# Second block: the value projections of all heads ahead of the head loop, tokens as rows

## The chip, the cores and the metric

One core of a Trainium2 chip runs the whole kernel in one launch. The metric is the device time of that launch in microseconds. TensorE (PE) does the matmuls, VectorE (DVE) and ScalarE (ACT) the elementwise work, SyncE (SP) and GpSimd (POOL) issue the DMAs. A matmul here takes a stationary tile of 128x128 and streams up to 512 columns past it.

## The reference, cut to what matters

Two transformer-like blocks run one after the other on 512 tokens of width 2048. The change lies in the second:

```
h = rms_norm(x, norm_g)
qa, ka, va, ga, qb, kb, vb, gb = split(h @ w_in)      # 8 parts, each 8 heads of 128
ya = stick_breaking_attention(qa, ka, va)             # per head, causal, blocks of 128 queries
yb = chunk_band_attention(norm(qb), norm(kb), vb)     # per head, 512 tokens, softmax with a bias
x  = x + concat(ya * silu(ga), yb * silu(gb)) @ w_out
```

`va` and `vb` are the value projections; no norm or nonlinearity stands between them and the attention weights, only the rms factor of each token.

## The kernel before, in words

All products are made of float32 split into a high and a low half; a product is three matmuls (high by high, high by low, low by high). A weight unit is 16 tiles of 128x128, 1 MB. SP loads it (`load`, `one_load`) into one of two raw buffers, ScalarE copies its high half (`hi`, L450, four pieces), VectorE subtracts the low half (`lo`, L893, four pieces), and TensorE runs `gemm`: 16 k-steps (k-tiles) of three matmuls of 512 columns into one of two PSUM banks, with the weights as stationary operand, so that the result has features as rows and tokens as columns. The next unit's halves are made while a unit runs; both must be there before its matmuls. `unit` counts finished units, `evac` emptied banks.

The first block ends with an output product of 16 units (`U_O1`). Then comes the second block's head loop (`d2_head` in each engine's program): 8 heads of 8 units each, in the order A queries, A keys, A values, A gate, B queries, B keys, B values, B gate. Each engine's order is written by hand; waits are semaphores. Between k-steps of `gemm` TensorE puts the head's attention matmuls: `scores` A after 2 k-steps of unit 3, `values` A in unit 5, a sum of squares (`b_ss`, 64-row halves folded by VectorE, L1475 to L1477) after 8 k-steps of units 5 and 6, scores B after 14 of unit 6, values B of the head before after 10 of unit 1.

Values come out of `gemm` with tokens as columns, but `values` needs tokens as rows. So VectorE turns them in 32x32 squares (`turn_values`, L1392), and SP sends them to DRAM and back in another order (`regroup`); ScalarE and VectorE then split them (`value_hi`, L796, `value_lo`, L1396). The attention weights of A and B take the same way (`turn_weights`, L1401 and L1403, `regroup`, `weight_hi`, L801, `weight_lo`, L1409): VectorE turns, SP writes to DRAM, waits for the landing, reads back, ScalarE copies, VectorE subtracts.

A's stick-breaking weights are made block by block: ScalarE takes Abs, Exp and Ln of the scores (L821 to L823), VectorE runs five operations with a scan in them (L1457 to L1462, called a stick below), ScalarE an Exp. B's queries and keys are normed: VectorE evacuates (L1473), ScalarE squares, VectorE folds, TensorE sums over the head, ScalarE takes the inverse root, VectorE scales (L1487 to L1490), ScalarE copies the high half, VectorE subtracts the low one (L1492); then come scores B.

The first block's gMLP has a value projection too, with four units that run the other way: activations stationary, weights streaming, tokens as rows, a bank for each 128 tokens.

Of the kernel before, what the change touches and what calls it, by code (L numbers as in the profile page):

```python
# [12 lines left out]
P = 128  # L13
S = 512
# [18 lines left out]
U_D2 = U_O1 + KT  # L33
U_O2 = U_D2 + 8 * DN
# [9 lines left out]
VALUES_AT = 12  # L44
LATE_VALUES_AT = 10
FIRST_VALUES_AT = 15
# [43 lines left out]
def build(nc, w, w_ab, xT, memT, rows_in, consts, negatives, params, ws_t, bs_b, ln_rows, rel, x1_dram, rows_dram, way_v, way_w, outT):  # L90
    with ExitStack() as ctx:
# [53 lines left out]
        QA, KA, VA, SGA = (tl(i) for i in (4, 5, 6, 8))  # L145
# [5 lines left out]
        QB, KBN, VBT, SGB, BIAS = (tl(i) for i in (18, 19, 20, 22, 23))  # L151
        PB = LB
        VTH, VTL = vtok_t[:, 0:S], vtok_t[:, S:2 * S]
        VTURN, VRAW = tl(7), tl(21)
# [34 lines left out]
        chunk_bank = [bank[1], pb[2], pb[3], pb[4]]  # L189

# [37 lines left out]
        def v3(a):  # L228
# [21 lines left out]
            turned v_turn va_in vb_in w_turn aw_in bp_in v_hi a_vtok a_hi a_lo a_z a_l a_x a_w a_wh a_wl a_o  # L250
# [8 lines left out]
        def _(sp):  # L259
# [180 lines left out]
        def _(act):  # L440
# [332 lines left out]
            hi(U_D2, U_D2 % 2)  # L773
# [9 lines left out]
            act.wait_ge(sem["unit"], U_D2)  # L783
            for k in range(12, KT - 1):
                x1_hi(k)
            act.wait_ge(sem["evac"], U_D2)
            x1_hi(KT - 1)
            o1_squares(KT - 1)
            hi(U_D2 + 1, (U_D2 + 1) % 2)
# [4 lines left out]
            def value_hi(ready, n):  # L794
                act.wait_ge(sem[ready], n)
                A(in_order(VTH, NB), by_row(VRAW, NB), ACT.Copy).then_inc(sem["v_hi"], 1)  # L796
# [6 lines left out]
            def d2_head(h, tail=True, last=False):  # L803
                u = 8 * h + U_D2
# [3 lines left out]

                if tail:
                    weight_hi("bp_in", 64 * h)  # L810

                for j in range(3):
                    next_hi(j)
                    if j < 2:
                        act.wait_ge(sem["evac"], u + (j + 1))
                        A([QH, KH][j], [QA, KA][j], ACT.Copy).then_inc(sem["a_hi"], 1)

                for i, c in enumerate(reversed(range(NB))):
# [5 lines left out]
                next_hi(3)  # L824
                for i, c in enumerate(reversed(range(NB))):
# [3 lines left out]
                sigmoid("g_y", 2 * h + 1, "g_sig")  # L829
                value_hi("va_in", 64 * h + 64)  # L830

                for j in range(2):
                    act.wait_ge(sem["evac"], u + (5 + j))
                    A(SQ[0:H, :], Y[0:H, :], ACT.Square)
                    A(E[0:H, :], Y[H:P, :], ACT.Square).then_inc(sem["b_sq"], 1)
                    if j == 0:
                        weight_hi("aw_in", 64 * h + 64)
                    next_hi(4 + j)

                    rsqrt(E, pb[5][:, :], -1.0 / P, "b_ss", 2 * h + j + 1, "b_r")  # L840
                    act.wait_ge(sem["b_n"], 2 * h + j + 1)
                    A([QH, KH][j], [QB, KBN][j], ACT.Copy).then_inc(sem["b_hi"], 1)
                for c in range(NB):
                    pc = PB[:, DO[c]:DO[c] + DNN[c]]
                    act.wait_ge(sem["b_max"], NB * h + c + 1)
                    A(pc, pc, ACT.Exp, bias=small[:, c:c + 1], accum_out=small[:, 4 + c:5 + c]).then_inc(sem["b_exp"], 1)
                next_hi(6)
                value_hi("vb_in", 64 * h + 64)
# [4 lines left out]
                if last:  # L853
# [13 lines left out]
                next_hi(7)  # L867
# [16 lines left out]
        def _(dve):  # L884
# [487 lines left out]
            lo(U_D2, U_D2 % 2)  # L1372
# [6 lines left out]
            lo(U_D2 + 1, (U_D2 + 1) % 2)  # L1379
# [8 lines left out]
            dve.wait_ge(sem["o1_st"], 16 * KT)  # L1388


            def turn_values(src):
                V.transpose(by_row(VTURN, NB), src).then_inc(sem["v_turn"], 1)  # L1392

            def value_lo(n, done):
                dve.wait_ge(sem["v_hi"], n)
                V.tensor_tensor(in_order(VTL, NB), by_row(VRAW, NB), in_order(VTH, NB).bitcast(F32), ALU.subtract)\  # L1396
                    .then_inc(sem[done], 1)

            def turn_weights(src, c):
                n = min(c + 1, NB - 1)  # L1400
                ins = V.transpose(by_row(SPB, SLOTS)[:, c:c + 3 * n - 2:3], src[:, DO[c]:DO[c] + n * P])  # L1401
                if c == NB - 1:
                    ins = V.transpose(by_row(SPB, SLOTS)[:, 7:8], src[:, DO[c] + n * P:DO[c] + DNN[c]])  # L1403
# [8 lines left out]
            def d2_head(h, tail=True, last=False):  # L1412
                u = 8 * h + U_D2
# [17 lines left out]
                if tail:  # L1431
                    gate_silu(2 * h, SGB)
                    weight_lo(4 * h - 2)

                for j, dst in enumerate((QA, KA, VA)):
                    unit(u + j)
                    V.scalar_tensor_tensor(dst, bank[slot(j)][:, :], SCALE if j == 0 else 1.0, R12, ALU.mult, ALU.mult)\  # L1437
                        .then_inc(sem["evac"], 1)
                    if j == 2:
                        dve.wait_ge(sem["evac"], u + 3)  # L1440
                        turn_values(VA)
                    next_lo(j)
                    if j < 2:
                        dve.wait_ge(sem["a_hi"], 2 * h + j + 1)
                        V.tensor_tensor([QL, KL][j], dst, [QH, KH][j].bitcast(F32), ALU.subtract).then_inc(sem["a_lo"], 1)
                    if j == 0 and tail:
                        dve.wait_ge(sem["b_o"], h)
                        out = (h + (DN - 1)) * S
                        out = big[:, bass.ds(out, S)] if not isinstance(out, int) else big[:, out:out + S]
                        V.tensor_tensor(out, pb[4][:, :], SGB, ALU.mult).then_inc(sem["mixed"], 1)  # L1450
                        dve.wait_ge(sem["mixed"], 2 * h + M1)

                for i, c in enumerate(reversed(range(NB))):
# [9 lines left out]
                gate_in(3, SGA)  # L1463
                next_lo(3)
                for i, c in enumerate(reversed(range(NB))):
                    dve.wait_ge(sem["a_w"], NB * h + i + 1)
                    ins = turn_weights(WB, c)
                ins.then_inc(sem["w_turn"], 1)
                gate_silu(2 * h + 1, SGA)
                value_lo(2 * h + 1, "a_vtok")  # L1470
# [613 lines left out]
```

## Time and profile before

| what | value |
|---|---|
| runs of the kernel before (3) | median 1888.71 us, 1887.75 to 1888.98 |
| the profiled execution | 1888.65 us, span 1887.0 us |
| granted TensorE clock, whole span | 1.000 |
| TensorE busy | 1880.1 us of the span |
| VectorE busy, ScalarE busy | 1203.0 us, 819.9 us |
| matmuls | 8912 |

The span runs from the first to the last instruction of the profile. Matmuls are pipelined and their ends are modelled: a row's duration of 0.39 us is longer than the step from one start to the next, so the step is what a matmul costs in a stream. "Idle before" in square brackets is time in which the engine stood still ahead of a row, with what ended it.

### The profile page before, as it was taken

The page shows a single profiled execution, that of the slowest core. Times are in us where ns is not written, and L with a number is a line of the kernel's source. Part 1 is how long each engine was busy: PE and PEld are TensorE (multiplying, and loading weights), DVE is VectorE, ACT ScalarE, POOL GpSimd, SP SyncE. Part 2 cuts the span into 40 slices and gives each one's busy share as a digit, 9 for nine tenths or more (in the row PEclk, how much of TensorE's full clock was granted, in tenths as well). Part 3 has the DMA queues.
Part 4 walks back from the last instruction along what each step waited for, and adds up shares of the span by engine and source line. Part 5 has one row for each costly group of instructions (what it writes and reads, how often), then busy time and mean ns, then how long its engine had stood idle before and what let it go on. Part 6 is the DMA issues. An engine that isn't in the chain of part 4 may idle for free.

```text
span 1887.0 us, 26887 instructions
## 1 busy us (share of the span) xinstructions
PE 1880.1 (100%) x8912; PEld 1564.5 (83%) x8912; DVE 1203.0 (64%) x2246; ACT 819.9 (43%) x1581; POOL 112.4 (6%) x172
## 2 busy tenths in 40 slices
PE   9999999999999999999999999999999999999999
PEld 8788888888888888888888888888888888888887
DVE  6565687788777865734467575757575757576333
ACT  5654444444444444533444343434343535354111
POOL 0100011101111010010000000000000000000100
PEclk9999999999999999999999999999999999999999
DMA  9722233223232212334433434343434333333441
GB/s 331 296 90 83 82 82 88 78 78 78 78 94 74 77 67 100 129 139 144 148 114 113 140 120 147 114 143 116 138 122 135 126 132 125 135 121 134 149 151 67
DMA packets 56146, 230.25 MB, mean 122 GB/s; under 512 B 7073, under 2 KB 23073, under 8 KB 35617
## 3 DMA queue, kind: packets, MB, share of 16 engines
q1 hardware_dynamic: 46224, 194.01, 29.2%
q0 software_dynamic: 9728, 35.49, 6.7%
q8 instruction: 30, 0.49, 0.1%
q14 instruction: 20, 0.16, 0.0%
q10 hardware_dynamic: 144, 0.10, 0.0%
HBM read 207.13 MB, written 22.45 MB: 122 GB/s over the span
## 4 chain that ended last, share of the span: by engine, by line
PE 93%; DVE 3%; DMA 2%; ACT 1%; issue 0%; SPq 0%; DVEq 0%; ACTq 0%
PE gemm L1582 80%; PE pb L1582 12%; DMA raw<-in_w 1%; DVE w_lo L893 1%; PE pb L1585 1%; DMA way_w<-scratch 1%; DMA scratch<-way_w 0%; DVE scratch L1460 0%; ACT w_hi L450 0%; DVE scratch L1461 0%; DVE scratch L1457 0%; DVE w_lo_t L1409 0%; DVE scratch L1401 0%; DVE scratch L1458 0%; SPq L306 0%
## 5 line engine op out<-in xcount | busy, mean ns | idle before, releaser
L1582 PE MATMUL gemm<-act_hi,w_hi 128*128 128x512 f32 x2304 | 918.6, 399 | 0.0
L1582 PE MATMUL gemm<-act_lo,w_hi 128*128 128x512 f32 x2320 | 903.0, 389 | 0.2 <-DVE w_lo L893 0.2
L1582 PE MATMUL gemm<-act_hi,w_lo 128*128 128x512 f32 x2304 | 899.1, 390 | 0.0
L1582 PEld LDWEIGHTS gemm<-act_hi,w_lo 128*128 128x128 f32 x2304 | 432.4, 188 | 92.9
L1582 PEld LDWEIGHTS gemm<-act_lo,w_hi 128*128 128x128 f32 x2320 | 436.5, 188 | 84.7 <-ACT w_hi L450 0.5
L450 ACT ACTIVATE w_hi<-raw 128x512 fp32r<-128x512 f32 x616 | 337.2, 619 | 379.9 <-PE gemm L1582 360.4
L1582 PEld LDWEIGHTS gemm<-act_hi,w_hi 128*128 128x128 f32 x2304 | 433.3, 188 | 82.1 <-issue 0.4
L893 DVE TENSOR_TENSOR w_lo<-raw,w_hi 128x512 fp32r<-128x512 f32 x624 | 399.1, 696 | 151.1 <-ACT w_hi L450 145.2
L1582 PEld LDWEIGHTS pb<-scratch 128*128 128x128 f32 x932 | 135.9, 192 | 27.2 <-DVE scratch L1264 5.9
L1582 PE MATMUL pb<-scratch 128*128 128x128 f32 (+3 forms) x932 | 141.8, 279 | 2.6 <-DVE scratch L908 1.7
L1437 DVE SCALAR_TENSOR_TENSOR scratch<-gemm,scratch 128x512 f32<-128x512 f32 x24 | 16.6, 692 | 95.9 <-PE gemm L1582 95.9
L390 POOL TENSOR_TENSOR scratch<-scratch,cst 128x256 f32<-128x256 f32 x56 | 47.6, 855 | 416.2 <-DVE scratch L1155 243.3
L457 ACT ACTIVATE scratch<-scratch 128x512 f32<-128x512 f32 x56 | 35.2, 628 | 79.0 <-DVE scratch L1104 44.0
L1103 DVE SCALAR_TENSOR_TENSOR scratch<-scratch,par 128x511 f32<-128x511 f32 (+2 forms) x72 | 54.0, 750 | 9.9 <-DVE scratch L1101 3.2
L469 ACT ACTIVATE scratch<-pb,eps 128x512 f32<-128x512 f32 x41 | 28.1, 686 | 69.6 <-PE pb L1582 69.6
L765 ACT ACTIVATE scratch<-big 128x512 f32 (+1 forms) x16 | 10.1, 632 | 108.3 <-DVE big L1351 108.3
L1351 DVE TENSOR_TENSOR big<-gemm,scratch 128x512 f32 (+1 forms) x16 | 11.0, 689 | 68.5 <-PE gemm L1582 68.5
L646 ACT ACTIVATE scratch<-pb 128x128 f32<-128x128 f32 x40 | 11.1, 278 | 91.0 <-PE pb L1582 90.6
L423 POOL DMA_DIRECT2D scratch<-in_rel x7 | 3.8, 540 | 638.7 <-DVE scratch L1500 638.7
L1409 DVE TENSOR_TENSOR w_lo_t<-scratch,w_hi_t 128x640 fp32r<-128x640 f32 x30 | 23.4, 822 | 27.1 <-ACT w_hi_t L801 27.1
L801 ACT ACTIVATE w_hi_t<-scratch 128x640 fp32r<-128x640 f32 x30 | 20.5, 731 | 42.7 <-DMA scratch<-way_w 42.7
L458 ACT ACTIVATE scratch<-scratch 128x512 f32<-128x512 f32 x56 | 35.4, 633 | 1.8
(299 smaller groups left out, 1658.1 us busy)
## 6 DMA issues: line engine op xcount, KB each, us to landing
raw<-in_w SPq DMA_DIRECT2D x154, 1024.0 KB, 4.8
way_w<-scratch SPq DMA_DIRECT2D x15, 640.0 KB, 5.0
scratch<-way_w SPq DMA_DIRECT2D x60, 160.0 KB, 3.1
scratch<-in_rows_in POOLq DMA_DIRECT2D x6, 1024.0 KB, 8.3
big<-in_xT POOLq DMA_DIRECT2D x4, 1024.0 KB, 7.8
scratch<-rows POOLq DMA_DIRECT2D x16, 256.0 KB, 6.1
scratch<-in_xT POOLq DMA_DIRECT2D x16, 256.0 KB, 2.9
x<-big POOLq DMA_DIRECT2D x16, 256.0 KB, 2.3
```

Source lines behind the costliest of these rows:

```text
L390: nc.gpsimd.tensor_tensor(v3(blk(ML, NB * (k % 2), 2)), pair(AT, 0), C[f"level{k}"].rearrange("p (c t) -> p c t", c=1).broadcast_to([P, 2, ...
L450: A(w_hi[slot][:, c], raw[slot][:, c], ACT.Copy).then_inc(sem["hi"], 1)
L457: st.then(A(E, SS, ACT.Exp, scale=-1.0))
L458: st.then(A(E, E, ACT.Ln, bias=1.0))
L469: st.then(A(dst, src, ACT.Ln, bias=eps[:, 0:1], scale=scale))
L801: A(in_order(WBH, SLOTS)[:, s], by_row(WB, SLOTS)[:, s], ACT.Copy).then_inc(sem["a_wh"], 1)
L893: V.tensor_tensor(w_lo[slot][:, c], raw[slot][:, c], w_hi[slot][:, c].bitcast(F32), ALU.subtract)\
L1103: st.then(V.scalar_tensor_tensor(Y[:, 3 - k:], SS[:, :S - 3 + k], tap(k), Y[:, 3 - k:], ALU.mult, ALU.add))
L1409: V.tensor_tensor(in_order(WBL, SLOTS)[:, s], by_row(WB, SLOTS)[:, s], in_order(WBH, SLOTS)[:, s].bitcast(F32), ALU.subtract).then_inc(sem ...
L1437: V.scalar_tensor_tensor(dst, bank[slot(j)][:, :], SCALE if j == 0 else 1.0, R12, ALU.mult, ALU.mult)\
L1582: return nc.tensor.matmul(out, a, b, start=start, stop=stop, skip_group_check=skip)
L1585: return nc.tensor.transpose(out, a, C["ident"])
```

## The change

The two value projections leave the head loop. A new stage of 16 units (`U_VP`) runs between the first block's output product and the head loop: four groups (A's values of heads 0 to 3, of 4 to 7, B's likewise), each of four units. In a unit (`value_unit`) the split activations are stationary and the weights stream, 512 columns for four heads at once; the result has tokens as rows, in four banks for four blocks of tokens, with two sets of four banks in turn. ScalarE empties a group's four banks into `big` with the rms factor of each token as scale (`R12C`, made by VectorE from the broadcast row). `big` held x1, whose stores must have landed.

The head loop has six units: A queries, A keys, B queries, B keys, A gate, B gate. Values are read from `big` when their head comes; their turning and their trips through DRAM go away. Scores A now stand after 5 k-steps of unit 2, the sums of squares after 8 of units 3 and 4, scores B after 14 of unit 4, values A after 4 of unit 5. VectorE evacuates B's queries between the second and the third stick, and the two gates are taken later. ScalarE's copies of A's weights, and VectorE's subtraction, stand ahead of the keys' norm. SP loads two units, sends A's weights round, loads three, sends B's round, and loads one.

```diff
-U_D2 = U_O1 + KT
-U_O2 = U_D2 + 8 * DN
+U_VP = U_O1 + KT
+U_D2 = U_VP + 4 * NB
+U_O2 = U_D2 + 6 * DN
-VALUES_AT = 12
+SCORES_AT = 5
+VALUES_AT = 4
...
 (SyncE, per head)
-                u = U_D2 + 8 * h + 4
+                u = U_D2 + 6 * h + 4
                 one_load(u)
                 one_load(u + 1)
-                sp.wait_ge(sem["v_turn"], 2 * h + 1)
-                regroup(VRAW, VTURN, way_v, 4 * h + 1, "va_in")
+                sp.wait_ge(sem["w_turn"], 2 * h + 1)
+                regroup(WB, SPB, way_w, 2 * h + 1, "aw_in")
                 one_load(u + 2)
                 one_load(u + 3)
-                sp.wait_ge(sem["w_turn"], 2 * h + 1)
-                regroup(WB, SPB, way_w, 4 * h + 2, "aw_in")
                 one_load(u + 4)
-                one_load(u + 5)
-                sp.wait_ge(sem["v_turn"], 2 * h + 2)
-                regroup(VRAW, VTURN, way_v, 4 * h + 3, "vb_in")
-                one_load(u + 6)
                 if h < DN - 1:
                     sp.wait_ge(sem["w_turn"], 2 * h + 2)
-                    regroup(WB, SPB, way_w, 4 * h + 4, "bp_in")
-                one_load(u + 7)
+                    regroup(WB, SPB, way_w, 2 * h + 2, "bp_in")
+                one_load(u + 5)
...
 (ScalarE, the new stage)
+            for n in range(4):
+                u = U_VP + 4 * n
+                for j in range(3):
+                    hi(u + j + 2, (u + j) % 2)
+                if n == 0:
+                    act.wait_ge(sem["o1_st"], 16 * KT)
+                    act.wait_ge(sem["act_lo"], 4 * KT)
+                    act.wait_ge(sem["r12c"], 1)
+                act.wait_ge(sem["unit"], u + 4)
+                heads = big[:, 4 * n * S:(4 * n + 4) * S].rearrange("p (h x) -> p h x", x=S)
+                for c in range(NB):
+                    A(heads[:, :, c * P:(c + 1) * P], v3(value_bank[n % 2][c][:, :]), ACT.Copy, scale=R12C[:, c:c + 1])\
+                        .then_inc(sem["evac"], 1)
+                hi(u + 5, (u + 3) % 2)
 (ScalarE, per head, the new order)
+                for j in range(2):
+                    act.wait_ge(sem["evac"], u + (j + 1))
+                    A([QH, KH][j], [QA, KA][j], ACT.Copy).then_inc(sem["a_hi"], 1)
                     next_hi(j)
...
+                value_hi(h)
                 (Abs, Exp and Ln of the four blocks of scores A)
+                weights_of(0, NB - 1)
+                weights_of(1, NB - 2)
+                next_hi(2)
+                fold_squares(0)
+                weights_of(2, 1)
+                weights_of(3, 0)
+                normed(0)
+                next_hi(3)
+                fold_squares(1)
+                weight_hi("aw_in", 64 * h + 64)
+                normed(1)
+                next_hi(4)
                 (Exp of the four blocks of scores B)
+                sigmoid("g_y", 2 * h + 1, "g_sig")
+                act.wait_ge(sem["a_o"], h + 1)
+                value_hi(h + DN)
...
 (VectorE, per head, the new order, after the two evacuations of A)
+                value_lo(h, 2 * h + 1, "a_vtok")
+                stick(0, NB - 1)
+                stick(1, NB - 2)
+                b_in(0)
+                stick(2, 1)
+                stick(3, 0)
+                folded(0)
+                for i, c in enumerate(reversed(range(NB))):
+                    dve.wait_ge(sem["a_w"], NB * h + i + 1)
+                    ins = turn_weights(WB[:, DO[c]:DO[c] + DNN[c]], c)
+                ins.then_inc(sem["w_turn"], 1)
+                next_lo(2)
+                normed(0)
+                b_in(1)
+                folded(1)
+                next_lo(3)
+                weight_lo(4 * h)
+                normed(1)
                 (bias and maxima of scores B)
+                gate_in(4, SGA)
+                next_lo(4)
+                gate_silu(2 * h + 1, SGA)
...
 (TensorE)
+            def value_unit(n, j):
+                u = U_VP + 4 * n + j
+                slot = u % 2
+                for q in range(4):
+                    k = 4 * j + q
+                    pe.wait_ge(sem["hi"], 4 * u + q + 1)
+                    pe.wait_ge(sem["lo"], 4 * u + q + 1)
...
+                    f = slice(q * S, (q + 1) * S)
+                    for c in range(NB):
...
+                        t = slice(k * S + c * P, k * S + (c + 1) * P)
+                        out = value_bank[n % 2][c][:, :]
+                        mm(out, act_hi[:, t], w_hi[slot][:, f], k == 0, False)
+                        mm(out, act_hi[:, t], w_lo[slot][:, f], False, False)
+                        ins = mm(out, act_lo[:, t], w_hi[slot][:, f], False, k == KT - 1)
...
-                d2(2)
-                d2(3, 0, 2)
+                d2(2, 0, SCORES_AT)
                 pe.wait_ge(sem["a_lo"], 2 * h + 2)
                 for c in reversed(range(NB)):
                     scores(c, QA, KA).then_inc(sem["a_z"], 1)
-                d2(3, 2)
-                d2(4)
+                d2(2, SCORES_AT)
                 for j in range(2):
-                    d2(5 + j, 0, 8)
+                    d2(3 + j, 0, 8)
                     pe.wait_ge(sem["b_sql"], 2 * h + j + 1)
                     mm(pb[5][:, :], sums[:, P:2 * P], SQH).then_inc(sem["b_ss"], 1)
                     if j == 0:
-                        d2(5, 8, values_at)
-                        (values A)
-                        d2(5, values_at)
+                        d2(3, 8)
                     else:
-                        d2(6, 8, 14)
+                        d2(4, 8, 14)
                         pe.wait_ge(sem["b_lo"], 2 * h + 2)
                         for c in range(NB):
                             scores(c, QB, KBN).then_inc(sem["b_sc"], 1)
-                        d2(6, 14)
+                        d2(4, 14)
+                d2(5, 0, VALUES_AT)
+                (values A)
```

Lines in round brackets stand for code that is left out or name its engine. In the host's preparation the value weights are laid out so that a unit's tile holds 512 columns for one k-tile.

## Rows read from the trace of the kernel before

**Rows 1.** Busy time by windows: stretch, us, then PE, PEld, DVE, ACT, POOL, PEclk, DMA.

```profile
979.00:1028.60 49.60, 48.72 (x223) 40.24 (x223) 36.51 (x69) 25.71 (x51) 0.00 (x0) 1.00 0.37 122
1123.60:1218.60 95.00, 95.00 (x434) 79.34 (x433) 61.11 (x115) 41.30 (x81) 0.54 (x1) 1.00 0.38 130
1313.60:1409.10 95.50, 95.33 (x434) 79.29 (x433) 61.09 (x115) 41.32 (x81) 0.54 (x1) 1.00 0.37 129
```

**Rows 2.** Waits of TensorE, 940 to 1712 us: total, times, longest.

```profile
PE pb L1582 <- DVE parts L1492: 0.7, 1, 0.7
PE pb L1582 <- DVE w_lo_t L1409: 0.2, 1, 0.2
PE pb L1582 <- DVE parts L1477: 0.2, 1, 0.2
```

**Rows 3.** The chain that ended last, in order of time: start, us, what.

```profile
97.64 8.16 PE pb L1582 x36
...
998.11 6.90 DMA way_w<-scratch
1006.35 3.52 DMA scratch<-way_w
...
1123.61 29.94 PE gemm L1582 x132
...
1171.79 1.79 PE pb L1582 x11
```

**Rows 4.** Timeline of TensorE in head 0: start, us, instruction, idle before.

```profile
1020.66 0.39 PE L1582 MATMUL gemm<-act_hi,w_lo 128*128 128x512 f32 x1
1021.22 0.50 PE L1582 MATMUL pb<-parts,sums 128*128 128x512 f32 x1 [0.17 <-DVE parts L1477]
1021.56 0.39 PE L1582 MATMUL gemm<-act_hi,w_hi 128*128 128x512 f32 x1
```

**Rows 5.** Timeline of ScalarE in a steady head.

```profile
1265.54 2.20 ACT L450 ACTIVATE w_hi<-raw 128x512 fp32r<-128x512 f32 x4 [8.16 <-PE gemm L1582]
1267.64 0.58 ACT L821 ACTIVATE scratch<-pb 128x512 f32<-128x512 f32 x1
...
1294.59 1.37 ACT L801 ACTIVATE w_hi_t<-scratch 128x640 fp32r<-128x640 f32 x2 [3.50 <-DMA scratch<-way_w]
```

**Rows 6.** Timeline of VectorE in the same head.

```profile
1269.58 0.69 DVE L1457 SCALAR_TENSOR_TENSOR scratch<-pb,scratch 128x512 f32<-128x512 f32 x1 [0.28 <-ACT scratch L823]
...
1275.53 0.42 DVE L1457 SCALAR_TENSOR_TENSOR scratch<-pb,scratch 128x256 f32<-128x256 f32 x1
...
1279.34 0.68 DVE L1423 TENSOR_TENSOR scratch<-gemm,scratch 128x512 f32<-128x512 f32 x1
...
1282.81 0.57 DVE L1401 STREAM_TRANSPOSE scratch<-scratch 128x384 f32<-128x384 f32 x1
...
1284.48 0.65 DVE L1429 TENSOR_TENSOR scratch<-scratch 128x512 f32<-128x512 f32 x1
...
1289.09 0.69 DVE L1473 TENSOR_TENSOR scratch<-gemm,scratch 128x512 f32<-128x512 f32 x1 [3.24 <-PE gemm L1582]
1291.12 0.68 DVE L1475 TENSOR_TENSOR parts<-scratch 64x512 fp32r<-64x512 f32 x1 [1.34 <-ACT scratch L835]
...
1295.36 1.56 DVE L1409 TENSOR_TENSOR w_lo_t<-scratch,w_hi_t 128x640 fp32r<-128x640 f32 x2 [2.23 <-ACT w_hi_t L801]
1296.84 2.49 DVE L893 TENSOR_TENSOR w_lo<-raw,w_hi 128x512 fp32r<-128x512 f32 x4
1299.30 0.49 DVE L1487 TENSOR_SCALAR scratch<-scratch,par 128x512 f32<-128x512 f32 x1
...
1301.22 0.69 DVE L1492 TENSOR_TENSOR parts<-scratch,parts 128x512 fp32r<-128x512 f32 x1 [0.70 <-ACT parts L842]
...
1309.32 0.75 DVE L1490 SCALAR_TENSOR_TENSOR scratch<-scratch,par 128x512 f32<-128x512 f32 x1
1310.77 0.69 DVE L1492 TENSOR_TENSOR parts<-scratch,parts 128x512 fp32r<-128x512 f32 x1 [0.70 <-ACT parts L842]
```

More of the change, by code:

```diff
@@ L823, in d2_head, with weights_of @@
                     A(lb, lb, ACT.Ln, bias=1.0).then_inc(sem["a_l"], 1)
-                next_hi(3)
-                for i, c in enumerate(reversed(range(NB))):
+                def weights_of(i, c):
                     wb = WB[:, DO[c]:DO[c] + DNN[c]]
@@ L1429, in gate_silu, with stick @@
                     st.then(V.tensor_tensor(dst, dst, E, ALU.mult))
[L1431 to L1453, printed above, removed]
+                def stick(i, c):
                     t = slice(DO[c], DO[c] + DNN[c])
@@ L1462, in d2_head, with b_in, folded @@
                     V.scalar_tensor_tensor(WB[:, own], WB[:, own], 0.0, C["hide"], ALU.min, ALU.add).then_inc(sem["a_x"], 1)
[L1463 to L1470, printed above, removed]
-                for j in range(2):
-                    unit(u + 4 + j)
-                    V.tensor_tensor(Y, bank[slot(4 + j)][:, :], R12, ALU.mult).then_inc(sem["evac"], 1)
+                def b_in(j):
+                    unit(u + 2 + j)
+                    V.tensor_tensor(Y, bank[slot(2 + j)][:, :], R12, ALU.mult).then_inc(sem["evac"], 1)
+                def folded(j):
                     dve.wait_ge(sem["b_sq"], 2 * h + j + 1)
@@ L1493, in d2_head @@
                         .then_inc(sem["b_lo"], 1)
+                if tail:
+                    gate_silu(2 * h, SGB)
+                    weight_lo(4 * h - 2)
+                for j, dst in enumerate((QA, KA)):
+                    unit(u + j)
+                    V.scalar_tensor_tensor(dst, bank[slot(j)][:, :], SCALE if j == 0 else 1.0, R12, ALU.mult, ALU.mult)\
+                        .then_inc(sem["evac"], 1)
+                    dve.wait_ge(sem["a_hi"], 2 * h + j + 1)
+                    V.tensor_tensor([QL, KL][j], dst, [QH, KH][j].bitcast(F32), ALU.subtract).then_inc(sem["a_lo"], 1)
+                    next_lo(j)
+                    if j == 0 and tail:
+                        dve.wait_ge(sem["b_o"], h)
+                        out = (h + (DN - 1)) * S
+                        out = big[:, bass.ds(out, S)] if not isinstance(out, int) else big[:, out:out + S]
+                        V.tensor_tensor(out, pb[4][:, :], SGB, ALU.mult).then_inc(sem["mixed"], 1)
+                        dve.wait_ge(sem["mixed"], 2 * h + M1)
+                value_lo(h, 2 * h + 1, "a_vtok")
[16 more added lines that the diff above has]
+                normed(1)
                 dve.wait_ge(sem["b_bias"], 16 * h + 16)
@@ new lines, in _ @@
+            for n in range(4):
+                if n == 1:
+                    pe.wait_ge(sem["o1_r1"], 1)
+                    pe.wait_ge(sem["o1_t"], 1)
+                if n >= 1:
+                    pe.wait_ge(sem["evac"], U_VP + 4 * (n - 1))
+                value_unit(n, 0)
+                if n == 0:
+                    pe.wait_ge(sem["o1_acc"], KT + 1)
+                    mm(pb[0][:, :], C["ones"], ACC1).then_inc(sem["o1_ss"], 1)
+                    mm(pb[1][:, :], C["ones"], ACC2).then_inc(sem["o1_ss"], 1)
+                for j in range(1, 4):
+                    value_unit(n, j)
@@ L1922, in d2, with d2_head @@
+            gemm(U_D2, U_D2 % 2, emptied=U_D2 - 4)
+            def d2_head(h, tail=True, last=False):
+                u = 6 * h + U_D2
                 def d2(j, k0=0, k1=KT):
-                    gemm(u + j, (U_D2 + j) % 2, k0, k1, free=j == 7)
+                    gemm(u + j, (U_D2 + j) % 2, k0, k1, free=j == 5)
                 def scores(c, q, k):
@@ L2043 @@
         interleave(dq, dk, dz, dv), interleave(gz, gu), tiles(np.concatenate([f["w_out"][0][gm:], f["w_out"][0][:gm]])),
-        interleave(*(w2[:, i * dn:(i + 1) * dn] for i in range(8))), tiles(f["w_out_2"][0])])
+        *(of_values(w2[:, i * dn + half * S:i * dn + (half + 1) * S]) for i in (2, 6) for half in range(2)),
+        interleave(*(w2[:, i * dn:(i + 1) * dn] for i in (0, 1, 4, 5, 3, 7))), tiles(f["w_out_2"][0])])
     assert w.shape[0] == U_END
```

159 lines of the change are left out of this document (72 added, 87 removed).

## The prediction

> **What bounds the kernel now.** I read first how much of each stretch TensorE is busy, by windows cut at the stages of the second block, then who TensorE waits for, then the steps of its chain, and last the order of VectorE and ScalarE inside one head. In a head of the second block TensorE is busy for all of the 95.00 us, at a granted clock of 1.00, VectorE for 61 us, ScalarE for 41 [rows 1]. Busy ends are modelled, so I check with steps: 132 matmuls of 512 columns took 29.94 us, 0.2268 us each, with no hole [rows 3]. From the end of the first block's output product to the last head TensorE waited three times, 1.1 us in all [rows 2]; head 3 was 0.5 us longer than its neighbours [rows 1]. So all that the second block's head loop can give back is about 1.6 us, unless matmuls go away or become faster.
>
> **Do they?** Before, 16 value units of 16 k-steps of 3 matmuls: 768. After, 4 groups of 4 units of 4 k-tiles, 4 token blocks and 3 products: 768, again 128x128 against 512 columns. The operands change sides (activations are now loaded, weights stream). The trace has that form, in the first block's gMLP value units: 36 matmuls in 8.16 us, 0.2267 us each [rows 3]. So the swap costs and gives nothing: 174 us of units move from the heads to a stage of their own. The Trainium skill ("TensorE: Matmul & The Clock Gate", Back-to-back issue gap) gives 512/2.4 + 2.5 = 216 ns for such a step; by that the 768 would be an estimated 8 us shorter, but both forms run at 227 here, and the sum doesn't use it.
>
> **The new value stage.** TensorE needs a unit's halves every 48 x 0.2268 = 10.9 us; splitting one costs ScalarE 2.20 [rows 5] and VectorE 2.49 us [rows 6]. At a group's end ScalarE adds four scaled copies out of PSUM, about 0.6 us each as the Abs of 128x512 out of PSUM [rows 5], while TensorE writes the other four banks. The stores of x1 that the copies wait for have a whole group, 43.5 us. The sums of squares move from 8.2 to 10.9 us into the stage, which eases them; the per-token scale is two VectorE operations of some 0.7 us. Everything is covered by TensorE's 43.5 us a group: cost 0.
>
> **What leaves the heads.** Per head two evacuations, two transposes, two weight splits and two DMA round trips of values: VectorE falls from 61.1 by 2 x 2.49 and about 4 x 0.7 to 53.3 us. But the head falls from 95.0 to 95.0 - 2 x 10.9 = 73.2 us on TensorE, and the serial path from scores A to scores B, in which almost nothing was removed, lies in less cover. Before, 38 + 4 + 12 + 6 = 60 k-steps (0.680 us each) stood between them; after, 11 + 8 + 8 + 8 + 6 = 41. Here the order on VectorE decides. I walk it with t = 0 at the start of unit 2 (B's queries).
>
> *TensorE wants:* 5 steps, scores A at 3.4 for 1.79 [rows 3], 11 steps, unit 3 at 12.7, 8 steps, first sum of squares at 18.1.
>
> *VectorE and ScalarE give:* keys evacuated at 0.2 to 0.9, copied by 1.6, subtracted by 2.3: in time for scores A. Then VectorE splits weights (2.49) and the value copy (0.69), to 5.4. ScalarE splits weights (2.20) and copies values, to 4.3; the first block of scores lands about then. From Abs to stick on VectorE took 1.94 us [rows 5, 6], so the sticks start at 6.3. The first two take 5.95 us, to 12.25; then B's queries are awaited (unit 2 ends at 12.7; a matmul's modelled 0.39 us outlasts its step by 0.17 [rows 4], so VectorE sees it at 12.9) and evacuated, 0.69, to 13.6; the last two sticks take 3.81, to 17.35; the fold is three operations of 0.68 [rows 6], to 19.4. **Wait 1: 19.4 - 18.1 = 1.3 us.** Before, VectorE was free when this fold came.
>
> *Next:* TensorE runs the sum at 19.4, a step, 16 k-steps, and wants the second sum at 30.6. VectorE from 19.3: turning the weights 1.67 (to 21.0), weight split 2.46 (23.4), B's queries normed, copied and subtracted 2.61 (26.0) [rows 6]. ScalarE, behind that copy and the end of unit 3 (25.2), splits weights to 27.6 and squares, 1.30 (the 2.03 us from evacuation to fold less the evacuation's 0.69 and a hop), to 28.9; the fold ends at 30.9. **Wait 2: 0.3 us.**
>
> *Next:* TensorE wants scores B 6 steps later, at 35.3. VectorE has in this order a weight split 2.46 (33.2), the low half of A's weights 1.48 (34.7), and the keys' norm, copy and subtraction 2.14 [rows 6], to 36.8. **Wait 3: 1.5 us.** The wait put in VectorE's queue is for A's turned weights: behind it stand the keys' norm and so scores B. Turned at 21.0, they need the trip through DRAM; in the steady head 10.1 us from the end of the turn (1284.48) to ScalarE's read (1294.59), in head 0 11.8 us from issue (998.11) to landing (1009.87) [rows 3, 5, 6]. That is 31.1 to 32.8; ScalarE then needs 1.37 for the copies [rows 5] and 1.3 for the norm's two passes (three took 1.94), which must end by 34.7: hidden in the steady case (33.8), 0.8 us late in the other. SP has issued unit 5's load long before and the next one stands behind the trip, so the queue is free when it starts. B's trip starts some 14 us after scores B, behind the maxima, the gate, a split and the turning, at about 52, and is wanted at 76.6 - 6 = 70: hidden.
>
> A wait also costs at restart: after head 0's sum of squares the next matmul came 0.34 us later instead of 0.227 [rows 4], 0.1 each.
>
> *Sum per head:* 1.3 + 0.3 + 1.5 + 3 x 0.1 = 3.4 us, eight heads 27.2. **Last head:** the probabilities stand behind gate A's sigmoid and two products, three ScalarE passes, 1.94 us, and two of VectorE at 0.69, 3.3 us if nothing covers them, 0 if all is covered; no row decides, I take the middle, 1.7. **Given back:** 1.6. Sum +27.3 on the profiled execution's 1888.65 us (span 1887.0; the median of the runs, 1888.71, is the same): **1916**.
>
> **Bounds.** The path from scores A to scores B is 33 us of summed rows. One us less of it per head gives 1888.65 + 8 x 2.4 + 0 - 1.6 = 1906; two less, 1898. With the slow DRAM trip, 8 x 4.2 + 3.3 - 1.6 = 35.3: 1924; 0.5 us more of hops per head, 1928.
>
> **Rivals.**
> *VectorE keeps up: no change.* It is the busiest after TensorE, yet at 53.3 of 73.2 us, 73%, has room. Then the three old waits go and none comes: 1888.65 - 1.6 = 1887, no change by the 0.2% (3.8 us) that a measurement of this kernel can tell. It decides if the first sum's path is 1.3 us shorter and the second's 1.8. Against it stands head 0: VectorE was busy 36.5 of 49.6 us there, 74%, and TensorE still waited for it, the sum starting 0.56 us after the matmul ahead instead of 0.227 [rows 1, 2, 4]. The Trainium skill ("Perfetto Trace Analysis", Identifying the Most-Contended Engine) takes occupancy as a fair measure for VectorE and looks for the highest; by that rule alone this rival is the forecast. It doesn't count an order with waits, which is what head 0 shows. Chance 0.12.
> *Part of it:* one wait is hidden by a hop that I priced too long, 8 x 1.5 or less: 1893 to 1900. Chance 0.1.
> *The DRAM trip is last:* it joins traffic as in head 0 or worse, each us beyond 32.1 is a us per head, 12 us trips give 1925 to 1935. Chance 0.07.
> *The swapped form streams faster:* at the granted clock of 1.00, 2.4 GHz, 512 columns are 0.2133 us, so at most 768 x (0.2268 - 0.2133) = 10 us, 1877 if no wait comes. The gMLP rows, the same form at 0.2267 us, speak against it. Chance 0.02.
> *The forecast,* three waits a head: 0.69, with 1900 to 1928 as its range.
>
> **Numbers.** 1916; the range 1900 to 1928 leaves out no change and faster (0.14) and about half of the tails, 0.2 together. Faster 0.02, same 0.12, slower 0.86.
>
> **What would show it.** The value stage: 768 matmuls at 0.227 us, no wait. A head: 76.6 us instead of 73.2. TensorE's waits: for VectorE's SQH line some 1.3 and 0.3 us a head, for the line of the keys' low half 1.5. Scores A must start without a wait. If sticks start earlier than 6 us into unit 2, or ScalarE's weight copies wait for DRAM until after 32, my walk is wrong in that place. A head of 73.2 us would refute it whole.

## The result and the profile after

The changed kernel takes **1918.3 us** (median of 4 runs, 1916.5 to 1919.0), the kernel before 1888.85 us (4 runs, 1887.75 to 1890.7): ratio 1.0153 [1.0136, 1.0171], slower by 29 us. Forecast were 1916 us, in 1900 to 1928. The profiled execution took 1916.5 us with a span of 1914.8; its span is 27.8 us longer than that of before. TensorE's first matmul that belongs to the change (the first product of the second block) shows where each profile stands when the change begins, in before and in after:

```profile
944.41 0.39 PE L1582 MATMUL gemm<-act_hi,w_hi 128*128 128x512 f32 x1
943.32 0.39 PE L1611 MATMUL pb<-w_hi,act_hi 128*128 128x512 f32 x1
```

The part ahead of the change, which is the same in both kernels, took 1.1 us less in this profile of after. From the change on, after is 28.9 us longer. Below, "from the change on" is counted in this way.

TensorE's waits in the whole profile of after (total, times, longest) answer to [rows 2]:

```profile
PE pb L1611 <- DVE parts L1483: 11.7, 8, 1.5
PE pb L1611 <- DVE parts L1473: 8.5, 8, 1.1
PE pb L1611 <- DVE scratch L931: 1.7, 1, 1.7
PE gemm L1611 <- DVE big L1374: 1.4, 1, 1.4
PE pb L1614 <- DVE scratch L1542: 1.2, 1, 1.2
PE gemm L1611 <- DVE w_lo L916: 0.4, 1, 0.4
```

The lines of after: L1483 is the subtraction that makes the low half of queries and keys (L1492 before), L1473 the last subtraction of a fold of squares (L1477 before), L1374 the evacuation of an O1 unit with the residual, L1542 the last head's probabilities. L931 and L916 lie in the kernel's first 90 us, where before had 2.2 us for the same two causes. So there are two new waits of all eight heads and two single ones. This view counts an idle time from a matmul's modelled end, so it shows each wait some 0.16 us shorter than the steps do, and it leaves out wait 2 below, of which only 0.1 us is left by that reading.

Windows of the value stage and of one head of after (stretch, us, then PE, PEld, DVE, ACT, POOL, PEclk, DMA) answer to [rows 1]:

```profile
947.00:1120.00 173.00, 173.00 (x759) 142.52 (x760) 47.01 (x75) 46.29 (x83) 1.09 (x2) 1.00 0.28 101
1223.00:1299.72 76.72, 74.06 (x337) 61.20 (x337) 53.37 (x103) 36.92 (x73) 0.54 (x1) 1.00 0.36 120
```

The value stage has no hole once it runs. A stretch of its chain (start, us, what) gives 0.2267 us a matmul, as the gMLP rows did [rows 3]:

```profile
990.52 44.88 PE pb L1611 x198
```

A head takes 76.72 us, and VectorE is busy for 53.37 of them. Before, a head took 95.00; less 2 x 10.88 for the value units that left it would be 73.24. So 3.48 us of every head are new, and TensorE's timeline shows where (start, us, instruction, idle before it):

```profile
1219.43 0.39 PE L1611 MATMUL gemm<-act_hi,w_hi 128*128 128x512 f32 x1
...
1222.84 1.74 PE L1611 MATMUL pb<-parts 128*128 128x512 f32 x9
...
1237.38 0.39 PE L1611 MATMUL gemm<-act_hi,w_lo 128*128 128x512 f32 x1
1238.83 0.50 PE L1611 MATMUL pb<-parts,sums 128*128 128x512 f32 x1 [1.06 <-DVE parts L1473]
1239.16 0.39 PE L1611 MATMUL gemm<-act_hi,w_hi 128*128 128x512 f32 x1
...
1249.84 0.39 PE L1611 MATMUL gemm<-act_hi,w_lo 128*128 128x512 f32 x1
1250.34 0.49 PE L1611 MATMUL pb<-parts,sums 128*128 128x512 f32 x1
...
1254.53 0.39 PE L1611 MATMUL gemm<-act_hi,w_lo 128*128 128x512 f32 x1
1256.39 0.49 PE L1611 MATMUL pb<-scratch 128*128 128x128 f32 x2 [1.48 <-DVE parts L1483]
```

Read the starts, since the ends are modelled: a step without a wait is 0.227 us. Scores A (1222.84) start five k-steps after unit 2 (1219.43), without a wait. The first sum of squares starts 1.45 us after the matmul ahead of it, so **wait 1** is 1.22 us; the second 0.50 after, **wait 2** 0.27; scores B 1.86 after, **wait 3** 1.63. After each sum the next matmul comes 0.33 us later, 0.11 more than a step, a restart. Scores B have one too. From their start to the next product they take 1.91 us here (to 1258.30), and 1.79 in the run below with the whole order in a head mended, where TensorE doesn't wait for them. First the row of after, then two of that run:

```profile
1258.30 0.39 PE L1611 MATMUL gemm<-act_hi,w_hi 128*128 128x512 f32 x1
```

```profile
1250.69 0.38 PE L1611 MATMUL pb<-scratch 128*128 128x128 f32 x2
...
1252.48 0.39 PE L1611 MATMUL gemm<-act_hi,w_hi 128*128 128x512 f32 x1
```

Three waits and three restarts make 3.45 us of the 3.48.

VectorE in the same head shows what stands ahead of these three points; two rows of ScalarE (ACT) are put between by their time:

```profile
1225.67 0.69 DVE L1458 SCALAR_TENSOR_TENSOR scratch<-pb,scratch 128x512 f32<-128x512 f32 x1 [0.87 <-ACT scratch L847]
...
1232.36 0.69 DVE L1467 TENSOR_TENSOR scratch<-gemm,scratch 128x512 f32<-128x512 f32 x1 [0.66 <-PE gemm L1611]
1232.97 0.41 DVE L1458 SCALAR_TENSOR_TENSOR scratch<-pb,scratch 128x256 f32<-128x256 f32 x1
...
1238.09 0.68 DVE L1473 TENSOR_TENSOR parts<-scratch,parts 64x512 fp32r<-64x512 f32 x1
...
1240.48 2.45 DVE L916 TENSOR_TENSOR w_lo<-raw,w_hi 128x512 fp32r<-128x512 f32 x4
...
1244.89 2.20 ACT L448 ACTIVATE w_hi<-raw 128x512 fp32r<-128x512 f32 x4 [0.17 <-PE gemm L1611]
...
1248.28 0.68 DVE L1471 TENSOR_TENSOR parts<-scratch 64x512 fp32r<-64x512 f32 x1 [2.23 <-ACT scratch L824]
...
1250.32 2.50 DVE L916 TENSOR_TENSOR w_lo<-raw,w_hi 128x512 fp32r<-128x512 f32 x4
1250.88 0.69 ACT L467 ACTIVATE scratch<-pb,eps 128x512 f32<-128x512 f32 x1 [1.24 <-PE pb L1611]
1252.74 1.55 DVE L1432 TENSOR_TENSOR w_lo_t<-scratch,w_hi_t 128x640 fp32r<-128x640 f32 x2
1254.21 0.74 DVE L1481 SCALAR_TENSOR_TENSOR scratch<-scratch,par 128x512 f32<-128x512 f32 x1
1255.65 0.69 DVE L1483 TENSOR_TENSOR parts<-scratch,parts 128x512 fp32r<-128x512 f32 x1 [0.70 <-ACT parts L829]
```

The fold ends at 1238.77 and the sum starts at 1238.83; the keys' low half ends at 1256.34 and scores B start at 1256.39. From the evacuation of B's queries (1232.36) to the end of the first fold VectorE is never idle: the last two sticks stand there, which nobody needs yet. Ahead of the second fold (1248.28) VectorE is idle for 2.23 us. It waits for the keys' squares, which stand on ScalarE behind the copies of a weight unit (1244.89, 2.20 us); at this point ScalarE's order is what comes last. Ahead of the keys' norm (1254.21) stand a split of the next unit's weights and the low half of A's. ScalarE was idle for 1.24 us ahead of the keys' inverse root (1250.88), so there VectorE's order comes last.

### The profile page after: what moved, and what is told of

Same layout as the page of the kernel before. It is cut to its first block, busy times and chain, and to the rows that moved or that the text cites. A ratio compares the mean times of both kernels' runs of the same rounds, so it can differ in the third digit from the quotient of the medians.

```text
span 1914.8 us, 26775 instructions
## 1 busy us (share of the span) xinstructions
PE 1885.3 (98%) x8912; PEld 1563.4 (82%) x8912; DVE 1182.4 (62%) x2216; ACT 828.5 (43%) x1597; POOL 112.1 (6%) x172
## 3 DMA queue, kind: packets, MB, share of 16 engines
q1 hardware_dynamic: 34704, 185.61, 27.8%
## 4 chain that ended last, share of the span: by engine, by line
PE 86%; DVE 7%; ACT 3%; DMA 3%; issue 1%; SPq 0%; POOL 0%; DVEq 0%; ACTq 0%
PE gemm L1611 68%; PE pb L1611 17%; DMA raw<-in_w 2%; DVE w_lo L916 2%; ACT w_hi L448 1%; PE pb L1614 1%; DVE w_lo_t L1432 1%; DMA scratch<-in_negatives 1%; DVE scratch L1472 1%; DVE scratch L1461 0%; DVE act_lo L1385 0%; ACT scratch L506 0%; DVE parts L1473 0%; DVE parts L1471 0%; DVE scratch L1462 0%
## 5 line engine op out<-in xcount | busy, mean ns | idle before, releaser
L1611 PE MATMUL gemm<-act_hi,w_hi 128*128 128x512 f32 x2048 | 818.7, 400 | 0.0
L1611 PE MATMUL gemm<-act_lo,w_hi 128*128 128x512 f32 x2064 | 803.2, 389 | 0.4 <-DVE w_lo L916 0.4
L1611 PE MATMUL gemm<-act_hi,w_lo 128*128 128x512 f32 x2048 | 799.8, 391 | 0.0
L916 DVE TENSOR_TENSOR w_lo<-raw,w_hi 128x512 fp32r<-128x512 f32 x624 | 398.9, 695 | 277.3 <-ACT w_hi L448 273.1
L1611 PEld LDWEIGHTS gemm<-act_hi,w_lo 128*128 128x128 f32 x2048 | 384.3, 188 | 82.9
L1611 PEld LDWEIGHTS gemm<-act_lo,w_hi 128*128 128x128 f32 x2064 | 388.4, 188 | 73.9 <-ACT w_hi L448 0.7
L1611 PEld LDWEIGHTS gemm<-act_hi,w_hi 128*128 128x128 f32 x2048 | 385.2, 188 | 71.8 <-issue 0.2
L1611 PE MATMUL pb<-w_hi,act_hi 128*128 128x512 f32 x240 | 93.8, 391 | 0.0
L1611 PE MATMUL pb<-w_hi,act_lo 128*128 128x512 f32 x240 | 93.4, 389 | 0.0
L1611 PE MATMUL pb<-w_lo,act_hi 128*128 128x512 f32 x240 | 93.4, 389 | 0.0
L836 ACT ACTIVATE parts<-scratch 128x512 fp32r<-128x512 f32 x16 | 10.1, 632 | 108.9 <-DVE scratch L1492 108.9
L763 ACT ACTIVATE scratch<-big 128x512 f32 (+1 forms) x16 | 10.1, 632 | 108.3 <-DVE big L1374 108.3
L1374 DVE TENSOR_TENSOR big<-gemm,scratch 128x512 f32 (+1 forms) x16 | 11.0, 687 | 68.5 <-PE gemm L1611 68.5
L1611 PEld LDWEIGHTS pb<-w_hi,act_hi 128*128 128x128 f32 x240 | 45.1, 188 | 9.6 <-issue 0.2
```

The source lines that it names most:

```text
L763: A(SQ, x1, ACT.Square)
L916: V.tensor_tensor(w_lo[slot][:, c], raw[slot][:, c], w_hi[slot][:, c].bitcast(F32), ALU.subtract)\
L1374: V.tensor_tensor(x1, bank[u0 % 2][:, :], blk(XIN, NB * j, NB), ALU.add).then_inc(sem["evac"], 1)
L1611: return nc.tensor.matmul(out, a, b, start=start, stop=stop, skip_group_check=skip)
```

## The experiments

The theory is the forecast's: three waits on a serial path through VectorE and ScalarE, set by the order in their queues and not by how much they have to do. The runs that move VectorE's work move ScalarE's passes with it; none moves one engine's order alone. Each time below is a median with its ratio to the kernel before on the same chip.

### The keys' norm ahead of two weight splits

```diff
 (VectorE)   folded(1)
+            normed(1)
             next_lo(3)
             weight_lo(4 * h)
-            normed(1)
 (ScalarE)   fold_squares(1)
-            weight_hi("aw_in", 64 * h + 64)
             normed(1)
+            weight_hi("aw_in", 64 * h + 64)
```

> The keys' norm stands ahead of unit 5's weight split and of the low half of A's weights on VectorE, and ahead of the copies of A's weights on ScalarE. Theory (a serial order between scores A and scores B): the keys' low half is ready some 0.3 us before TensorE wants scores B, so the third wait of 1.6 us a head goes and the other two stay: 8 x 1.64 = 13 us less, 1905. Rival (VectorE has too much to do for six units): the work is the same, so the wait comes back elsewhere and the time stays at 1916 to 1919.

Measured: 1905.15 us, 1.0081 [1.0064, 1.0098]. TensorE's waits from 1100 to 1900 us:

```profile
PE pb L1611 <- DVE parts L1473: 8.5, 8, 1.1
PE pb L1614 <- DVE scratch L1542: 2.3, 1, 2.3
```

The wait for the keys' half is gone from all heads, wait 1 stands as it was. 8 x 1.63 = 13.0 us and eight restarts of 0.11 come back, and the last head gives 1.1 of them away again, since its probabilities now come later (2.3 in place of 1.2). That makes 12.8 us, and from the change on the profile is 12.8 us shorter than after's. So wait 3 hangs on what stands ahead of the keys' norm. The run moves ScalarE's copies of A's weights too; that VectorE's two splits were what came last rests on the rows of after above, where ScalarE stood idle.

### The first fold ahead of the last stick

```diff
 (VectorE)   stick(2, 1)
-            stick(3, 0)
             folded(0)
+            stick(3, 0)
 (ScalarE)   weights_of(1, NB - 2)
-            next_hi(2)
             fold_squares(0)
+            next_hi(2)
```

> The fold of B's queries stands ahead of the last stick, and their squares ahead of unit 4's weight copies. Theory (one serial path whose length sets the head): the first wait of 1.2 us goes, but the second fold ends where it did, so the second wait grows from 0.27 to about 1.4 and the third stays: 0 to 2 us less in all, 1916 to 1918. Rival (each wait has its own cause and price, as my sum added them): 8 x 1.3 = 11 us less, 1907.

Measured: 1914.87 us, 1.0134 [1.0117, 1.0151]: a little below what the theory gave, far from the rival's 1907. Waits from 1100 to 1720 us, and TensorE's timeline at the two sums and at scores B of one head:

```profile
PE pb L1611 <- DVE parts L1483: 11.6, 8, 1.5
PE pb L1611 <- DVE parts L1473: 9.5, 8, 1.2
```

```profile
1314.65 0.39 PE L1611 MATMUL pb<-parts,sums 128*128 128x512 f32 x1
...
1325.53 0.39 PE L1611 MATMUL gemm<-act_hi,w_lo 128*128 128x512 f32 x1
1327.11 0.50 PE L1611 MATMUL pb<-parts,sums 128*128 128x512 f32 x1 [1.19 <-DVE parts L1473]
...
1333.16 0.49 PE L1611 MATMUL pb<-scratch 128*128 128x128 f32 x2 [1.46 <-DVE parts L1483]
```

The L1473 line still counts eight waits, but they are other ones: the first sum no longer waits (it starts a plain step of 0.23 us behind the matmul ahead of it), the second now waits 1.58 - 0.23 = 1.35 us in place of 0.27. A head gains 1.22 + 0.11 - 1.08 = 0.25 us, eight of them 2; from the change on the profile is 2.3 us shorter than after's. The waits are one path: what TensorE doesn't lose at the first point, it reaches the second too early by.

### The DRAM trip made longer

One more copy of A's turned weights to DRAM is put ahead of the trip that is used; the last two lines only count it.

```diff
 (SyncE)     sp.wait_ge(sem["w_turn"], 2 * h + 1)
-            regroup(WB, SPB, way_w, 2 * h + 1, "aw_in")
+            sp.dma_start(way_w, SPB).then_inc(sem["turned"], 16)
+            sp.wait_ge(sem["turned"], 16 * (3 * h + 1))
+            regroup(WB, SPB, way_w, 3 * h + 2, "aw_in")
             ...
-                regroup(WB, SPB, way_w, 2 * h + 2, "bp_in")
+                regroup(WB, SPB, way_w, 3 * h + 3, "bp_in")
```

> A's turned weights are written to DRAM twice, one after the other, before they are read back: the trip is some 3 us longer in each head. Theory: the trip has more than 2 us to spare behind VectorE's order, so the time stays within 2 us of 1918. Rival (the trip through DRAM is what the keys' norm really waits for): up to 8 x 2.9 = 23 us more.

Measured: 1920.17 us, 1.0166 [1.0149, 1.0183]; the interval overlaps that of after. In after, the weights were turned at 1240.48, and ScalarE's copies of them, which in this head didn't wait for the trip (in others 0.4 us at most), started at 1248.27, 7.8 us later. They ended at 1249.64, and VectorE took them up at 1252.74. The landing of the write to DRAM had become quicker. The page's DMA issues (KB each, median us to landing) of after:

```profile
way_w<-scratch SPq DMA_DIRECT2D x15, 640.0 KB, 2.9
```

Before it was 5.0. With the second copy ScalarE does wait for the trip, but TensorE's waits grow by 0.6 us in all. ScalarE in the same head, then TensorE's waits for the keys' half:

```profile
1252.12 1.37 ACT L815 ACTIVATE w_hi_t<-scratch 128x640 fp32r<-128x640 f32 x2 [3.14 <-DMA scratch<-way_w]
```

```profile
PE pb L1613 <- DVE parts L1485: 12.3, 8, 2.1
```

So the trip is not what is last in the changed kernel, and it has some 3 us to spare. They are nearly used up here: in one of the eight heads (longest wait 2.1) the lengthened trip was last. From the change on the profile is 2.2 us longer than after's; 0.6 us are the waits, and in the same head the clock fell, as the last section shows.

### The first value unit in an order that spares the waited bank

At the start of the value stage, TensorE waits for VectorE's evacuation of the last O1 unit, since the fourth token block's products go to that unit's bank. Here the first unit does the three other blocks of its four k-tiles first.

```diff
-                for q in range(4): (and for c in range(NB) within)
+                order = [(q, c) for q in range(4) for c in range(NB)]
+                if n == 0 and j == 0:
+                    order = [(q, c) for q in range(4) for c in range(3)] + [(q, 3) for q in range(4)]
+                for q, c in order:
```

> In the first unit of the value stage the fourth token block's matmuls come after those of the other three, so that its bank is wanted 6 us later. Theory (the stage itself costs nothing but a wait for that bank): 1.6 us less, 1916.7, and no wait of TensorE left in the stage. Rival (the wait only moves to the next unit, because VectorE is late with the operands): 1918.

Measured: 1916.27 us, 1.0138 [1.0121, 1.0155]. TensorE has no wait left from 940 to 1100 us, where in after's timeline it had this one:

```profile
945.13 0.39 PE L1611 MATMUL gemm<-w_hi,act_lo 128*128 128x512 f32 x1
946.95 0.50 PE L1611 MATMUL gemm<-w_hi,act_hi 128*128 128x512 f32 x1 [1.44 <-DVE big L1374]
```

That step is 1.82 us, a wait of 1.6. The profiled span is 1915.1, not shorter than after's, because this execution waited longer for weights in its first 90 us:

```profile
PE gemm L1611 <- DVE w_lo L916: 2.4, 3, 1.4
```

2.4 us stand against 0.4 in after. From the change on, this profile is 1.8 us shorter than after's: the wait of 1.6 and its restart of 0.1 are gone. The medians (2.0 us apart, with intervals that overlap) agree and wouldn't prove it by themselves.

### The whole order in a head, with the change left in place

Every operation of the changed kernel is kept. VectorE and ScalarE do them in the order in which TensorE wants them: the first fold ahead of the last stick, the evacuation of B's keys between the two halves of B's queries, the second fold at once, a split, the keys' norm, then the low half of A's weights. ScalarE squares the queries and the keys ahead of the copies of a weight unit.

```diff
 (VectorE)   stick(2, 1)
-            stick(3, 0)
             folded(0)
+            stick(3, 0)
             (turning the weights)
             next_lo(2)
-            normed(0)
-            b_in(1)
+            normed(0, lambda: b_in(1))
             folded(1)
             next_lo(3)
-            weight_lo(4 * h)
             normed(1)
+            weight_lo(4 * h)
 (ScalarE)   weights_of(1, NB - 2)
+            fold_squares(0)
             next_hi(2)
-            fold_squares(0)
             (the last two blocks' weights)
             normed(0)
+            fold_squares(1)
             next_hi(3)
-            fold_squares(1)
+            normed(1)
             weight_hi("aw_in", 64 * h + 64)
-            normed(1)
```

The second argument of `normed` is done between the norm and the subtraction of the low half.

> Only the order in a head is changed: the queries' fold ahead of the last stick; B's keys evacuated while ScalarE copies the queries, and squared ahead of unit 5's weight copies; the keys' norm ahead of the low half of A's weights. Theory (order, not amount): all three waits of a head go, by a margin of only some 0.3 us at the last, 8 x 3.45 = 27.6 us less, 1891. Rival (VectorE's amount of work bounds a head of six units): the waits move, and the time stays above 1905.

Measured: 1889.62 us, 1.0006 [0.9997, 1.0015]. One head, by windows, and all waits of TensorE from 1100 to 1900 us:

```profile
1219.00:1292.20 73.20, 73.20 (x338) 61.32 (x337) 53.44 (x103) 36.74 (x73) 0.54 (x1) 1.00 0.38 126
```

```profile
PE pb L1614 <- DVE scratch L1542: 1.2, 1, 1.2
```

This is the decisive run. VectorE is busy for 53.44 us of a head as in after (53.37), TensorE does the same matmuls, and the head is 73.2 us instead of 76.7: the whole loss of the heads was the order, on VectorE and ScalarE together. From the change on the profile is 1.0 us longer than before's, which is the value stage and the last head less what before waited. The Trainium skill ("Perfetto Trace Analysis", Identifying the Most-Contended Engine) takes VectorE's occupancy as a fair measure of how close the engine is to its roofline. Here the occupancy is 70% in the head that loses 3.5 us and 73% in the one that loses none, so it doesn't tell whether TensorE has to wait for the engine.

### The order, the value start and the last head together

To the order above are added the first value unit's order, and in the last head VectorE makes the probabilities ahead of gate A's products, the first of which waits for ScalarE's sigmoid:

```diff
 (VectorE)   gate_in(4, SGA)
             next_lo(4)
-            (gate A's products)
+            if not last: (gate A's products)
             (the probabilities)
+            if last: (gate A's products)
```

> The order of the run before this one, the value stage's first unit with its fourth token block last, and in the last head the probabilities ahead of gate A's products. Theory: 27.6 + 1.7 + 1.4 us less than the changed kernel, 1887.6, within 0.2 per cent of the kernel before, since TensorE's own work is the same. Rival (the stage or the swapped form costs TensorE something itself): over 1893.

Measured: 1887.52 us (11 runs), 0.9993 [0.9984, 1.0002]. From 900 to 1900 us TensorE has no wait at all. It is the best version found. By the medians it is no different from the kernel before. By the profiles it is 2.2 us shorter from the change on, since TensorE's matmuls are the same and before had some 2 us of holes in this part.

### Two more operations, on the path and off it

Two unused VectorE products of 128x512 (about 0.7 us each) are added to each head, once ahead of the first fold, once behind gate B's evacuation. They add work and change no result.

```diff
 (on the path)    stick(3, 0)
+                 st.then(V.tensor_tensor(tl(21), QA, KA, ALU.mult))   (twice)
                  folded(0)
 (off the path)   gate_in(5, SGB)
+                 st.then(V.tensor_tensor(tl(21), QA, KA, ALU.mult))   (twice)
```

> The changed kernel with two more VectorE products of 128x512 per head, 0.72 us each, ahead of the queries' fold; their result is not used. Theory (serial path): 8 x 1.44 = 11.5 us more, 1930. Rival (idle time on VectorE, 30 per cent of a head, takes them up): no change.

> The same two products, but right behind gate B's evacuation, where VectorE has 2.5 us of idle time and nothing of scores A or B is behind it soon. Theory: no change, within 1 us of 1918. Rival (any VectorE work costs, because VectorE's load is the bound): 11 us more, as in the run with the products on the path.

Measured: on the path 1933.99 us, 1.0249 [1.0233, 1.0265]; off it 1917.84 us, 1.0156 [1.0140, 1.0172]. The same work costs nothing in one place and 16 us in the other. But 16 is 4 more than was expected. On the path, the waits view gives

```profile
PE pb L1613 <- DVE parts L1473: 20.1, 8, 2.5
```

that is 11.6 us more than in after, as expected. The rest lies behind the wait. TensorE's timeline and two windows of a head:

```profile
1319.10 0.39 PE L1613 MATMUL gemm<-act_hi,w_lo 128*128 128x512 f32 x1
1322.01 0.80 PE L1613 MATMUL pb<-parts,sums 128*128 128x512 f32 x1 [2.52 <-DVE parts L1473]
1322.60 0.63 PE L1613 MATMUL gemm<-act_hi,w_hi 128*128 128x512 f32 x1
1323.03 0.63 PE L1613 MATMUL gemm<-act_lo,w_hi 128*128 128x512 f32 x1
```

```profile
1315.00:1319.00 4.00, 4.00 (x19) 3.31 (x18) 3.73 (x11) 3.22 (x7) 0.00 (x0) 1.00 0.00 0
1322.00:1324.70 2.70, 2.69 (x6) 2.15 (x7) 2.70 (x7) 1.32 (x2) 0.00 (x0) 0.50 0.07 27
```

After the wait the granted clock is 0.50, that is 1.2 GHz instead of 2.4, and a step takes 0.43 us in place of 0.227. This came in two of the eight heads at 1.4 us each, 2.8 us in all. 11.6 + 2.8 = 14.4, and from the change on the profile is 14.4 us longer than after's. The spans differ by 16.5, since the part ahead of the change, which is the same in both, took 2.1 us more in this profile.

## Why the prediction was right, point by point

**The swapped form, nothing: right.** 0.2267 us a matmul in the value stage. The rival of a faster stream has no row that bears it out, and neither has the estimate from the Trainium skill ("TensorE: Matmul & The Clock Gate", Back-to-back issue gap), whose 216 ns that section gives for an isolated matmul and not for a stream.

**The value stage, nothing: mis-sized by 1.7 us.** Inside, it runs without a hole. At its start TensorE waits 1.6 us, and 0.1 at restart, for a bank that VectorE has yet to evacuate. The step failed since I walked the stage's supply of operands and not who still held its banks.

**The walk of a head: right.** With t = 0 at 1219.43:

| | forecast | measured |
|---|---|---|
| sticks start | 6.3 | 6.2 |
| B's queries evacuated from | 12.9 | 12.9 |
| first sum wanted, started | 18.1, 19.4 | 18.2, 19.4 |
| second sum wanted, started | 30.6, 30.9 | 30.6, 30.9 |
| scores B wanted, started | 35.3, 36.8 | 35.3, 37.0 |
| waits 1, 2, 3 | 1.3, 0.3, 1.5 | 1.22, 0.27, 1.63 |
| head | 76.6 | 76.7 |

Three restarts of 0.11 show, three of 0.1 were forecast. Three waits and three restarts make 3.45 us a head, 27.6 for eight, forecast 27.2.

**The DRAM trip, hidden: right, with more room than I gave it.** I took 10.1 to 11.8 us from [rows 3, 5, 6]; it took 7.8, and the write landed in 2.9 us instead of 5.0. That no 1 MB load is under way when it starts, as the walk said, would explain it; this was argued and not tried.

**The last head, 1.7: 1.4 measured** by steps (1.2 by the waits). The middle between two bounds stood for a step that no row decided. **Given back, 1.6: about 2.1** by the steps of before, by which each wait reads longer and three restarts of 0.11 count.

**Sum:** 27.6 + 1.7 + 1.4 - 2.1 = 28.6 us, where the profiles differ by 28.9 from the change on and the forecast was 27.3. So 0.3 us is not assigned. The forecast's sum missed the measured terms by 1.3 us: it was too low by the unforeseen 1.7 and by 0.4 for the heads, and too high by 0.3 for the last head and by 0.5 for what is given back. That the spans differ by only 27.8, close to the forecast, is luck: the part ahead of the change was 1.1 us shorter in this profile of after.

**The rivals.** "VectorE keeps up" was wrong at the place that was named: it has room on average, and none ahead of the first fold and the keys' norm; ahead of the second fold it is idle and waits for ScalarE. The run with the order mended shows that the rival could have held, with the same work. "Part of it" would have needed one shorter hop; the run with the fold first shows that the first wait can't vanish alone when the next lies 11 us behind it on the same path; the run with the keys first shows that the last one can. "The DRAM trip is last" is refuted by the run that lengthens it.

**What the range missed in kind.** Nothing in it allowed for the granted clock. In the changed kernel's profile it never fell; the run with two more operations is the one where I forecast without it, and there the error was 4 us.

## What to carry to other kernels

When work of the bounding engine moves out of a loop, list what that work was covering: the serial path that stays in the loop now runs against a shorter cover, and a path that was covered before can end up 3 us too long while no engine gets any busier. Walk the order of the engines on that path against the points at which the bounding engine wants its results, and put work that is wanted late behind work that is wanted soon; cure all the points on a path at once, since the first one cured hands most of its wait to the next. A stage that moves also takes over the banks of what ran ahead of it: ask who still holds each of them at its first write.

## What was not expected of the hardware

TensorE's clock fell after some single waits that are little longer than those of the changed kernel. After the waits of the changed kernel, up to 1.9 us by steps, the granted clock stayed 1.00. After steps of 2.5 us, in one head of the run with the longer trip, and 2.9 us, in two of eight heads of the run with two more operations, it fell from 2.4 to 1.2 GHz. After a step of 2.65 us, at the probabilities of the last head of the run with the keys first, it didn't fall. The windows behind the steps of 2.5 and of 2.65 us, with the clock third from the end:

```profile
1641.40:1645.40 4.00, 3.93 (x14) 3.45 (x15) 3.28 (x10) 0.00 (x0) 0.00 (x0) 0.61 0.04 16
1718.95:1722.95 4.00, 4.00 (x23) 3.48 (x24) 4.00 (x8) 3.31 (x8) 0.00 (x0) 1.00 0.17 72
```

With that, and with six more heads at 2.9 us and no fall, the length of the wait alone doesn't decide; what else does stays open. The Trainium skill ("TensorE: Matmul & The Clock Gate", HAM oscillation) tells of loops in which every wait for a DMA makes the next matmuls start at half the clock. The trace agrees that the clock falls after a wait and that steps then take 0.43 in place of 0.227 us, here after a wait for VectorE.

The part ahead of the change is the same work in all of these kernels, yet its length differs by 2.7 us between their profiles: the change begins at 943.3 us in after, at 944.4 in before, at 945.4 in the run with two more operations on the path and at 946.0 in the run with everything together. TensorE's waits for weights at the start came to 0.2 to 2.9 us in them. A difference of 1 or 2 us between two profiles is therefore read from the change on, and not from the spans.
